# First mixture of experts: every weight block on two column tiles of 64

## What is computed

```python
D_MODEL = 1024; SEQ = 256; D_FF = 2816; N_EXPERTS = 8; TOP_K = 2
...
def moe_swiglu(x, w_router, b_router, w_in, w_out):
    ...
    logits = (x2 @ w_router).astype(jnp.float32) + b_router.astype(jnp.float32)
    top_vals, top_idx = lax.top_k(logits, TOP_K)
    gates = jax.nn.softmax(top_vals, axis=-1)
    ...
    def expert_block(args):
        xb, e = args
        h = xb @ w_in[e]
        return (jax.nn.silu(h[:, :D_FF]) * h[:, D_FF:]) @ w_out[e]
    ...
    y = jnp.zeros_like(x2).at[slot_tok].add((ys * slot_gate[:, None]).astype(x2.dtype))
```

## Time and profile before

| | us |
|---|---|
| median of 3 runs | 2015.55 (2015.4 to 2020.21) |
| span of the profiled execution | 2010.8 |
| PE busy in it | 1903.9 (95%) |
| weight loads (PEld) busy | 1510.0 |
| VectorE, ScalarE, GpSimd busy | 516.2, 247.7, 156.6 |
| mixture of 8 experts, first to last expert matmul | 558.7 to 1331.4 |
| line 1116 (input chunks), PE busy | 478.1, 9856 records |
| line 1135 (output chunks), PE busy | 234.0, 4928 records |
| mean rate of the DMAs over the span | 248 GB/s |

### The profile page before, as it was taken

One profiled execution on the slowest core, in us unless ns is written; L12 is line 12 of the kernel. 1 busy time (PEld: TensorE's weight loads), 2 busy tenths in 40 slices (PEclk: granted clock), 3 DMA queues, 4 the chain that ended last, 5 costly groups with the idle time before them and its releaser, 6 DMA issues.

```text
span 2010.8 us, 48118 instructions
## 1 busy us (share of the span) xinstructions
PE 1903.9 (95%) x22384; PEld 1510.0 (75%) x22384; DVE 516.2 (26%) x1215; ACT 247.7 (12%) x633; POOL 156.6 (8%) x303
## 2 busy tenths in 40 slices
PE   8999999999999999999999999989999999999775
PEld 7758885667499899999999999978756777754321
DVE  2641000232411101010101010035675433242223
ACT  2320000032101000000000000002223212110000
POOL 0000000100008300000000000016540000000000
PEclk9999999999999999999999999989999999999988
DMA  7225443421478989898999999872221007759996
GB/s 310 84 88 188 164 155 117 169 105 69 167 295 336 373 341 368 330 387 338 366 362 356 363 343 383 329 294 75 84 74 64 33 33 296 292 236 427 426 426 283
DMA packets 50340, 499.29 MB, mean 248 GB/s; under 512 B 5688, under 2 KB 14416, under 8 KB 15696
## 3 DMA queue, kind: packets, MB, share of 16 engines
q1 hardware_dynamic: 40000, 490.11, 61.6%
q10 hardware_dynamic: 10128, 5.97, 1.0%
HBM read 494.99 MB, written 1.05 MB: 247 GB/s over the span
## 4 chain that ended last, share of the span: by engine, by line
PE 87%; DMA 6%; DVE 4%; issue 1%; ACT 1%; DVEq 0%; SPq 0%; ACTq 0%
PE pb L1116 24%; PE pb L1135 12%; PE pb L766 11%; PE pb L775 7%; PE pb L771 4%; PE pb L839 4%; PE pb L1012 3%; DMA ringbuf<-in_e2out 2%; PE pb L1271 2%; PE pb L1294 2%; PE pb L1560 2%; DMA arena<-in_e2in 2%; PE pb L1057 2%; DMA ringbuf<-in_e2in 2%; PE pb L901 2%; PE pb L1282 1%
## 5 line engine op out<-in xcount | busy, mean ns | idle before, releaser
L1116 PE MATMUL pb<-arena,ringbuf 128*64 128x80 f32 (+1 forms) x9856 | 478.1, 240 | 1.8 <-issue 1.5
L1116 PEld LDWEIGHTS pb<-arena,ringbuf 128*64 128x64 f32 (+1 forms) x9856 | 462.8, 145 | 19.9 <-issue 5.3
L1135 PE MATMUL pb<-arena,ringbuf 128*64 128x80 f32 (+1 forms) x4928 | 234.0, 240 | 8.8 <-issue 8.8
L1135 PEld LDWEIGHTS pb<-arena,ringbuf 128*64 128x64 f32 (+1 forms) x4928 | 229.5, 146 | 13.1 <-issue 10.8
L1622 DVE TENSOR_TENSOR arena<-arena,pb 128x160 f32<-128x160 f32 (+3 forms) x130 | 48.0, 369 | 675.3 <-ACT arena L2588 430.5
L766 PE MATMUL pb<-XT,ringbuf 128*128 128x256 f32 (+2 forms) x1104 | 203.0, 347 | 0.8 <-ACT XT L2391 0.8
L766 PEld LDWEIGHTS pb<-XT,ringbuf 128*128 128x128 f32 (+1 forms) x1104 | 181.4, 193 | 22.1 <-issue 2.1
L2391 ACT ACTIVATE arena<-pb 128x256 f32<-128x256 f32 (+5 forms) x164 | 68.7, 437 | 430.6 <-PE pb L1135 114.4
L775 PE MATMUL pb<-arena 64*64 64x64 f32 (+4 forms) x664 | 105.6, 322 | 6.8 <-DVE Y L1622 4.1
L2588 ACT ACTIVATE arena<-pb 128x160 f32<-128x160 f32 x88 | 26.7, 303 | 582.1 <-PE pb L1116 582.0
L775 PEld LDWEIGHTS pb<-arena 64*64 64x64 f32 (+4 forms) x664 | 51.5, 151 | 56.5 <-issue 28.8
(11 more groups left out here) (367 smaller groups left out, 1897.8 us busy)
## 6 DMA issues: line engine op xcount, KB each, us to landing
ringbuf<-in_ein SPq DMA_DIRECT2D x88, 2048.0 KB, 10.4
ringbuf<-in_eout SPq DMA_DIRECT2D x64, 1408.0 KB, 7.8
arena<-in_e2in SPq DMA_DIRECT2D x13, 2048.0 KB, 26.0
ringbuf<-in_e2in SPq DMA_DIRECT2D x12, 2048.0 KB, 35.1
ringbuf<-in_fin SPq DMA_DIRECT2D x11, 2048.0 KB, 8.4
ringbuf<-in_e2out SPq DMA_DIRECT2D x8, 2048.0 KB, 30.8
ringbuf<-in_wo SPq DMA_DIRECT2D x6, 2048.0 KB, 8.5
arena<-in_e2out SPq DMA_DIRECT2D x6, 2048.0 KB, 33.5
```

Of the source, the lines that this page charges most:

```text
L1116: ins = pe.matmul(PB[b][h_, t * C1:(t + 1) * C1], w3[:, k, t * 128 + h_.start:t * 128 + h_.stop], XG[e % 2][:, k, :], start=k == 0, stop=k ...
L1135: ins = pe.matmul(PB[d // 4][h_, (d % 4) * C1:(d % 4 + 1) * C1], w3[:, f, h_], HT[:, f, :], start=f == 0, stop=f == 21)
```

## The change

In the mixture of 8 experts no block is done `WHOLE` any more: `t` = 0 of every input chunk and the output chunks `d` = 0 and 4 become `HALF`, like the others. The same weights are multiplied by the same values, and the same partitions of the same banks are written. Nothing else changes; the instruction lists of VectorE, ScalarE, GpSimd and SyncE are the same.

```diff
@@ -1112,7 +1112,7 @@
                     for t in range(4):
                         for k in range(8):
-                            for h_ in HALF if t else WHOLE:
+                            for h_ in HALF:
                                 ins = pe.matmul(PB[b][h_, t * C1:(t + 1) * C1], w3[:, k, t * 128 + h_.start:t * 128 + h_.stop],
                                                 XG[e % 2][:, k, :], start=k == 0, stop=k == 7)
@@ -1131,7 +1131,7 @@
                     for f in range(22):
-                        for h_ in HALF if d % 4 else WHOLE:
+                        for h_ in HALF:
                             ins = pe.matmul(PB[d // 4][h_, (d % 4) * C1:(d % 4 + 1) * C1], w3[:, f, h_], HT[:, f, :], start=f == 0, stop=f == 21)
```

## The result

The changed kernel takes 2036.34 us (median of 4 runs, 2033.64 to 2043.22) where the kernel before takes 2016.02. The ratio is 1.0097, 95% interval 1.0079 to 1.0116. The forecast was 1902 us, with 1892 to 1932 as its range: it has the wrong sign. The profiled execution took 2033.64 us, its span 2031.8 us, against a span of 2010.8.

What follows compares the result with a forecast made beforehand. The prediction took PE's own work as the bound, with weight DMA about level after the change. Savings of 87.1 + 32.5 - 1.4 - 4 = 114.2 us take 2015.55 to 1901.3 us, stated as 1902, range 1892 to 1932.

Steps and rivals of the forecast that it cites:

- Terms 1 and 2: Mixture on PE: all-half input chunks save 87.1 us, two of eight output chunks per expert 32.5 us; together 119.6 us.
- The rule on 62 ns for a matmul: Skill page's sequencer bound on small matmuls: a pair of half passes would cost 124 ns and the change would lose.
- rival B: Added half-pass pairs in the mixture don't overlap, only shape changes go: 27 us saved, 1988 us; chance 0.03.
- Term 3: PE's 10.3 us of mixture waits without a cause in the trace grow with the number of instructions: 1.4 us more.
- Term 4: Whether weight DMAs keep up in the mixture: 423 GB/s needed, 415 to 428 delivered when fully busy; 4 us lost.
- rival A: Weight DMA becomes the mixture's bound, at 400 GB/s effective: 86 us saved, 1929 us; chance 0.20.
- rival C: Waits for DMA in the mixture lower PE's clock, half passes cost about 69 ns: slower, 2096 us; chance 0.02.
- Waits called issue near 12 us: Sign for the third term: PE's mixture waits for which the trace names no semaphore stay near 12 us.
- the stage near 658 us: Sign for the whole forecast: the mixture, from first to last expert matmul, takes near 658 us.

Runs made afterwards that it cites:

- e1: The changed kernel with each expert chunk's load bringing only an eighth of its columns, results wrong: 1883.46 us, ratio 0.9351 to the kernel before.
- e2: The kernel before with each expert chunk's load bringing only an eighth of its columns, results wrong: 1996.62 us, ratio 0.9913.
- e11: e1 with column tiles of 32 in place of 64 in the two changed lines, twice the passes, results wrong: 2264.06 us, one run.

## Where the prediction held and where it failed

**Terms 1 and 2 held.** Half passes in the new places cost what the old ones cost. In e1 the input chunks start 4.43 us apart and the output chunks 3.04 us, as the terms had it. The stages of e1 and e2 are 114.1 us apart, where the two terms said 119.6. The rule on 62 ns for a matmul was rightly set aside, and rival B, which would have left 27 us, is out.

**Term 3 failed.** It took the 10.3 us of "issue" waits as a small cost in proportion to the number of instructions, +1.4 us, at most +10.3. They were the first sign of a limit that the kernel had just reached, and such waits grow with the excess over the limit: they came to 117.9 us. A block of 128 passes lasted 6.18 us on PE before, the fetch 6.2 us where it was waited for; with 4.42 us of passes such a block comes 1.8 us late. Blocks were waited for 93 times, at 137 packets in the stage, and for 1.3 us on average. The rest of the stage's 794.6 - 641.8 = 152.8 us over e1 is around the waits. Between two of them a block's passes stretch over 4.65 us, not 4.42: the last pass before a wait lasts its whole 0.23 us with none behind it, some 0.23 us x 90 = 21 us. And the granted clock is 0.50, the 1.2 GHz level, for 3.4 us in five places, at 713.7, 846.8, 956.0, 1099.4 and 1283.7 us, each 0.2 to 0.9 us behind the end of a wait of 2.1 to 2.4 us, none in e1's stage; by the passes of the earlier trace rows that is some 5 x 1.7 = 8.5 us, an estimate. 117.9 + 21 + 8.5 is 147 of the 153 us.

**Term 4 was not put to the test.** No wait of PE for `ringbuf` is listed, but in a stage of 794.6 us the weights need only 276.8 MB / 794.6 us = 348 GB/s, not 423. Whether the full rate would do for a stage of 655 us, and so whether rival A would have come, no run shows. The weights' traffic did decide, but by delaying instructions, not data. The prediction looked for what shares the DMA engines with TensorE's data and left out what shares them with its instructions.

**The rivals.** Rival A has not happened, and rival C's clock only as a small part of the loss. The slower outcome came by a mechanism that none of them named. Its signs were there: waits without a semaphore, at an instruction count that the change raises by 14%, and an instruction queue in the page whose packets and PE's instructions give 249 to a block. The clearest stands in the trace of the kernel before: counted in PE's records from the first of its "issue" waits, the others lie at 127, 508, 1906, 3557, 5462, 5844, 7749, 8129, 8893, 9654 and 11559, always within 3 of a whole multiple of 127, though its chunks have 112, 88 or 44 passes.

**What would show it.** "Waits called issue near 12 us" and the stage near 658 us were the right tests: with 118 and 794.6 us they pointed at term 3 at once.

## What to carry to other kernels

Splitting a matmul into two column tiles of 64 took a pass here from some 113 ns to 69 ns for the pair, and doubled its instructions. Before counting on the gain, compare the time in which TensorE uses up a block of instructions (here 128 passes) with the time in which a block comes, here 3.7 us with nearly idle DMA engines and often 6.2 us beside the full traffic of weights; what is paid is about the larger of the two. A mix of whole and half blocks that seems to leave TensorE time on the table can be near the point at which both are equal, and a few "issue" waits of 1 to 2 us, one block or a multiple of it apart, say that it has been reached.

## What the runs showed of the hardware that was not expected

- A block of 256 TensorE instructions comes in 3.7 us beside 35 to 48 GB/s of weights (e11) and in 6.2 us, where it is waited for, beside the full traffic of weights (356 GB/s in the stretch shown); at about half the traffic within 4.4 us in all but some 14 of 137 cases. Smaller weight packets (8 and 4 KB for 16), four loads for one, or one load fewer in the queue leave the 6.2 us as they are.
- From start to start, passes with column tiles of 32 follow one another every (2.42 - 0.23) us / 127 = 17.2 ns (e11), with 64 every 34.5 ns, whole ones every 112 to 115 ns, all at a granted clock of 1.00.
- The loads of 128 partitions cut into 112 + 16 or 120 + 8 partitions move 195 to 243 GB/s in stretches of 20 us with a DMA share of 0.79 to 1.01, in place of 415 to 428 at 1.00; cut into four by columns, the kernel loses less than 1% more.
